# Four places in SBUF for the inner values of an MLP, one for each chunk

## The chip, the cores and the metric

The kernel runs on one core of one Trainium2 chip. The metric is the device time of one execution in microseconds; the kernel before takes 2590.83 us, the median of three runs (2590.58 to 2592.93).

## What is computed

Two transformer-like blocks follow each other on 256 tokens of width 2048, all in float32. The change touches only the MLP at the end of the first block:

```
def sq_relu_mlp(h, w_in, w_out):
    return jnp.square(jax.nn.relu(h @ w_in)) @ w_out
...
    h2 = modulate(rmsnorm(x, norm2_g[i]), sh2, sc2)
    x = x + gt2 * sq_relu_mlp(h2, w_mlp_in[i], w_mlp_out[i])
```

`w_mlp_in` is 2048 x 8192 and `w_mlp_out` is 8192 x 2048. The squared values between the two products (256 tokens x 8192) are called the inner values here. Around the MLP stand a modulation, gated linear attention, a Fourier mixer and output projections before it, and a second block (convolution mixers and a gated MLP) after it.

## The kernel before

**Products in three parts.** Most products are done in TensorE's faster float32 form (`float32r`), with both operands split into a high and a low part: `whi` and `wlo` for the weights, `hh` and `hl` (or `mh` and `ml`) for the activations. One tile of a product is three matmuls: whi by hi (line 289), wlo by hi (line 291), whi by lo (line 293). The weight tile (128 x 128) is the stationary operand, the activations (128 partitions x 256 tokens) are the moving one. This is `feature_piece`. Where the output is wanted with tokens on the partitions, `token_piece` (lines 309, 310, 311) makes the activations stationary and moves 512 columns of `whi` or `wlo`. A few groups use plain float32 from the raw weights (`plain_group`, line 346).

**Weights.** SP's queue streams weights from HBM into the ring `raw` in pieces of 1 MB. ScalarE copies each half of a slot to `whi` (`hi_piece`, line 247), VectorE subtracts to get `wlo` (`lo_piece`, line 257), and TensorE waits for `lo_n` before it uses a piece. `used` frees the `whi`/`wlo` slot again.

**The MLP.** It is done in four chunks of 2048 inner values. A chunk has an in-stage (4 groups of 512 outputs, moving `hh` and `hl`) and an out-stage (4 groups of 512 outputs, moving the inner values `mh` and `ml`). A group is 16 k-tiles x 4 output tiles x 3 matmuls, 192 matmuls of 256 columns, accumulated in one of two PSUM buffers `acc`. After an in-group ScalarE takes the relu of the sums (line 889), VectorE squares (line 1379), ScalarE writes the high part to `mh` (line 891, semaphore `hhi_ok`) and VectorE the low part to `ml` (line 1382, semaphore `hid_ok`). The out-stage waits at its first group for `hid_ok`, inner group by inner group (line 1954). VectorE adds each out-group to `xT` (line 1297). The order is written out by hand: each engine's program runs through the chunks and groups in the same order.

**Where things lie.** Tensors are put one after the other, each starting at a multiple of 32 bytes. By the sizes of the tensors in front of them, `region_h` (with `hh`, `hl`) and `region_a` (with `mh`, `ml` and others that live at other times) start at 32 bytes modulo 128 in each partition. Each k-tile of 256 values is 1024 bytes, so every k-tile of `hh`, `hl`, `mh` and `ml` starts at 32 modulo 128. `oh`, `ol`, `yfh`, `yfl` and `hf` do so too. `whi` starts at 16 and `wlo` at 80 modulo 128 (both are taken 4 words into their tensor), and each 128-column tile keeps that. `dh` and `dl` (the second block's MLP) stand 24 words into `region_a`, at 0 modulo 128.

Of the kernel before, what the change touches and what calls it, by code (L numbers as in the profile page):

```python
# [4 lines left out]
P = 128  # L5
D = 2048
NT = 256
KT = D // P
# [81 lines left out]
def build(nc, ins, out):  # L90
    f32, f32r, u32 = mybir.dt.float32, mybir.dt.float32r, mybir.dt.uint32
    ALU, ACT = mybir.AluOpType, mybir.ActivationFunctionType
# [3 lines left out]
    with ctx:  # L96
# [6 lines left out]
        def overlay(hold, nbytes, *tensors):  # L103

            made = []
            for group in tensors:
# [9 lines left out]
        tmp = sb("tmp", [P, 2, 4 * NT])  # L116
# [23 lines left out]
            "region_h", 32768,  # L140
            [("hh", [P, KT, NT], f32r), ("hl", [P, KT, NT], f32r)],
            [("xN", [P, 2, D], f32), ("gN", [P, 2, D], f32)])
        (ch, cl, sqx, sqc, lab, keb, tq, state, dft, smid, mh, ml, _, dh, dl, hf) = overlay(
            "region_a", 32768 + 512,
            [("ch", [P, KT, NT], f32r), ("cl", [P, KT, NT], f32r)],
            [("sqx", [P, KT, NT], f32), ("sqc", [P, KT, NT], f32)],
# [1 line left out]
             ("state", [P, 2, HEADS, DV], f32), ("dft", [P, 2, DFT_COLS], f32),  # L148
             ("smid", [P, HEADS, DV], f32)],
            [("mh", [P, KT, NT], f32r), ("ml", [P, KT, NT], f32r)],  # L150
            [("behind", [P, 24], f32), ("dh", [P, KT, NT], f32r), ("dl", [P, KT, NT], f32r)],
            [("hf", [P, KT, NT], f32)])

# [33 lines left out]
        mask_w = [con2[:, (4 + d) * P:(5 + d) * P] for d in range(2)]  # L187
        half_w = [con2[:, 6 * P + 2 * d:6 * P + 2 * d + 2] for d in range(2)]
        tiles = lambda ap: ap.rearrange("p (t n) -> p t n", n=NT)
        pcol = lambda name, i=0, n=1: par[:, COL[name] + i:COL[name] + i + n]  # L190


# [490 lines left out]
        def _(act):  # L683
            act.dma_start(par[:, 2 * KT:NPARAM], ins["par"][:, 2 * KT:NPARAM]).then_inc(S["par_in"], 16)
            act.dma_start(con[:, :], ins["con"]).then_inc(S["con_in"], 16)
            st = Turn()
# [194 lines left out]
            for c in range(0, MLP_CHUNKS):  # L881
                for g in range(4):
                    n = 4 * c + g
                    if n:
                        C(st)
                        group_done(act, st)
                    else:
                        act.wait_ge(S["f_used"], 4)
                    nc.scalar.activation(tmp[:, 0, :], acc[g % 2][:, :], ACT.Relu).then_inc(S["relu_ok"], 1)
                    act.wait_ge(S["rsq_ok"], n + 1)  # L890
                    nc.scalar.activation(mh[:, 4 * g:4 * g + 4, :], tiles(tmp[:, 1, :]), ACT.Copy)\
                        .then_inc(S["hhi_ok"], 1)
                for g in range(4):
                    C(st)
                    if c == MLP_CHUNKS - 1:
                        mix_quad(g)
# [166 lines left out]
        def _(dve):  # L1063
# [304 lines left out]
            for c in range(0, MLP_CHUNKS):  # L1368
                for g in range(4):
                    n = 4 * c + g  # L1370
                    if n:
                        C()
                        group_done(dve, st)
                    else:
                        dve.wait_ge(S["f_used"], 4)
                    if c == 0:
                        late_out(dve, st, mp[1], st.e)
                    dve.wait_ge(S["relu_ok"], n + 1)
                    nc.vector.scalar_tensor_tensor(tmp[:, 1, :], acc[g % 2][:, :], 0.0, tmp[:, 0, :],
                                                   ALU.max, ALU.mult).then_inc(S["rsq_ok"], 1)  # L1380
                    dve.wait_ge(S["hhi_ok"], n + 1)
                    nc.vector.tensor_tensor(ml[:, 4 * g:4 * g + 4, :], tiles(tmp[:, 1, :]),
                                            mh[:, 4 * g:4 * g + 4, :].bitcast(f32), ALU.subtract)\
                        .then_inc(S["hid_ok"], 1)
                for g in range(4):
                    if c == MLP_CHUNKS - 1 and g:
                        C(2)
                        mix_lo(g - 1)
                        C(2)
                        mix_sums(g - 1)  # L1390
                        C(4)
                    else:
                        C()
                    group_done(dve, st)
                    if c + g == 0:
                        late_out(dve, st, mp[1], st.e)
                        dve.wait_ge(S["mo_ok"], 24)
                    add_scaled(g % 2, 4 * g, 3 * KT).then_inc(acc_free[g % 2], 1)
# [347 lines left out]
        def _(pe):  # L1746
# [196 lines left out]
            for c in range(0, MLP_CHUNKS):  # L1943
                for g in range(4):
                    if c + g == 0:
                        plain_group(pe, st, 0, hf, 0, n2_plain, lambda s: None, 0)
                    else:
                        mm_feature(pe, st, g % 2, hh, hl, 0, each=n2_ready if c + g == 1 else None,
                                   free=(S["rsq_ok"], 4 * c + g - 1) if g >= 2 else None)
                    if c == 0:  # L1950
                        late_turn(pe, st, mp[1])
                for g in range(4):
                    mm_feature(pe, st, g % 2, mh, ml, 1, free=(S["rsq_ok"], 4 * c + g + 3) if g < 2 else None,
                               ready=(lambda s: pe.wait_ge(S["hid_ok"], 4 * c + s + 1)) if g == 0 else None)
                    if c + g == 0:
                        late_turn(pe, st, mp[1])
                        assert st.t == 16
# [191 lines left out]
```

## Time and profile before

| | |
|---|---|
| median of three timed runs | 2590.83 us |
| the profiled execution | 2592.11 us |
| its span (first to last instruction) | 2590.3 us |
| TensorE matmul busy | 2537.2 us (98%) |
| weight loads busy | 2378.3 us (92%) |
| VectorE, ScalarE busy | 64%, 44% |
| mean granted TensorE clock | 0.993 |

Matmuls are pipelined and overlap in the records: one of 256 columns is drawn 277 to 281 ns long, but the next starts long before it ends. What a matmul costs in a stream is the distance from one start to the next. The views give it: where a line of the source view has n matmuls of one line, first and last start, the distance of the last and first start divided by n-1 is the time of one whole round of three matmuls, called a triple below.

### The profile page before, as it was taken

What the parts mean: (1) busy time and instruction counts of PE and PEld (TensorE: products, weight loads), DVE (VectorE), ACT (ScalarE), POOL (GpSimd) and SP (SyncE); (2) the same over time, 40 slices, a digit from 0 to 9 for tenths busy, and PEclk for the clock granted to TensorE, in tenths of its full rate; (3) what the DMA queues carried; (4) which work ended last, traced back from release to release, by engine and by line L of the source; (5) the groups of instructions that cost most, each with busy time, mean ns of one, the idle gap of its engine ahead of it and who ended that gap; (6) DMA issues with size and microseconds to landing.
All of it is one profiled execution on the core that took longest, in us unless ns stands there. A gap on an engine that the chain in (4) does not pass through costs nothing.

```text
span 2590.3 us, 42561 instructions
## 1 busy us (share of the span) xinstructions
PE 2537.2 (98%) x18912; PEld 2378.3 (92%) x18912; DVE 1658.1 (64%) x1999; ACT 1132.6 (44%) x1299; POOL 11.2 (0%) x24
## 2 busy tenths in 40 slices
PE   6999999999999999999999999999999999999998
PEld 3688799999998999999999999999899889988996
DVE  5366666677785755555555579776677556764775
ACT  3322565544444434434434552054455435543553
POOL 0000000000000000000000000000000000000000
PEclk8999999999999999999999999999999999999999
DMA  9976565588885755555555555454455555555553
GB/s 395 361 254 229 209 218 207 202 296 290 304 292 202 278 190 186 194 192 185 194 193 184 190 183 179 147 179 170 151 185 196 196 194 187 188 195 184 190 183 110
DMA packets 77223, 547.89 MB, mean 212 GB/s; under 512 B 8848, under 2 KB 8976, under 8 KB 12272
## 3 DMA queue, kind: packets, MB, share of 16 engines
q1 hardware_dynamic: 74304, 533.53, 57.7%
q0 software_dynamic: 2448, 11.14, 1.1%
q8 instruction: 148, 2.42, 0.4%
q10 hardware_dynamic: 288, 0.50, 0.1%
q14 instruction: 35, 0.29, 0.0%
HBM read 539.90 MB, written 5.24 MB: 210 GB/s over the span
## 4 chain that ended last, share of the span: by engine, by line
PE 96%; DVE 2%; ACT 1%; DMA 1%; issue 0%; SPq 0%; DVEq 0%; ACTq 0%
PE acc L289 23%; PE acc L293 22%; PE acc L291 22%; PE acc L346 5%; PE acc L309 5%; PE acc L310 5%; PE acc L311 5%; PE mp L376 1%; PE mp L309 1%; PE mp L311 1%; PE mp L310 1%; DMA raw<-in_w_mod 1%; PE mp L435 0%; PE mp L498 0%; DVE macc L420 0%; PE mp L1866 0%
## 5 line engine op out<-in xcount | busy, mean ns | idle before, releaser
L257 DVE TENSOR_TENSOR wlo<-raw,whi 128x1024 fp32r<-128x1024 f32 x773 | 934.9, 1222 | 679.4 <-ACT whi L247 677.7
L247 ACT ACTIVATE whi<-raw 128x1024 fp32r<-128x1024 f32 x773 | 812.1, 1058 | 1171.9 <-PE acc L293 873.3
L293 PE MATMUL acc<-hl,whi 128*128 128x256 f32 x3296 | 922.6, 280 | 0.0
L289 PE MATMUL acc<-hh,whi 128*128 128x256 f32 x3296 | 919.4, 279 | 0.0
L291 PE MATMUL acc<-hh,wlo 128*128 128x256 f32 x3296 | 915.2, 278 | 0.0
L289 PEld LDWEIGHTS acc<-hh,whi 128*128 128x128 f32 x3296 | 622.5, 189 | 4.6 <-issue 3.0
L293 PEld LDWEIGHTS acc<-hl,whi 128*128 128x128 f32 x3296 | 618.8, 188 | 0.0
L291 PEld LDWEIGHTS acc<-hh,wlo 128*128 128x128 f32 x3296 | 616.7, 187 | 0.5
L293 PE MATMUL acc<-ml,whi 128*128 128x256 f32 x1536 | 430.1, 280 | 0.0
L289 PE MATMUL acc<-mh,whi 128*128 128x256 f32 x1536 | 426.4, 278 | 0.0
L291 PE MATMUL acc<-mh,wlo 128*128 128x256 f32 x1536 | 426.4, 278 | 0.0
L289 PEld LDWEIGHTS acc<-mh,whi 128*128 128x128 f32 x1536 | 290.3, 189 | 0.3 <-issue 0.2
L293 PEld LDWEIGHTS acc<-ml,whi 128*128 128x128 f32 x1536 | 288.4, 188 | 0.0
L291 PEld LDWEIGHTS acc<-mh,wlo 128*128 128x128 f32 x1536 | 287.3, 187 | 0.1
L420 DVE SCALAR_TENSOR_TENSOR macc<-raw,csl,macc 128x512 f32<-128x512 f32 x240 | 180.2, 751 | 10.9 <-DMA raw<-in_w_mod 2.9
L346 PE MATMUL acc<-hf,raw 128*128 128x256 f32 x640 | 140.6, 382 | 7.7 <-ACT hf L987 4.1
L346 PEld LDWEIGHTS acc<-hf,raw 128*128 128x128 f32 x640 | 122.5, 192 | 25.3 <-issue 8.4
L310 PE MATMUL acc<-wlo,dh 128*128 128x512 f32 x352 | 139.3, 396 | 0.0
L309 PE MATMUL acc<-whi,dh 128*128 128x512 f32 x352 | 139.0, 395 | 0.0
L311 PE MATMUL acc<-whi,dl 128*128 128x512 f32 x352 | 138.9, 395 | 0.0
L1670 DVE SCALAR_TENSOR_TENSOR up<-um,par,up 128x255 f32<-128x255 f32 (+1 forms) x176 | 73.3, 478 | 25.7 <-ACT up L1010 24.9
L309 PE MATMUL acc<-whi,hh 128*128 128x512 f32 x192 | 80.0, 417 | 2.4 <-DVE hl L547 2.4
(319 smaller groups left out, 2181.4 us busy)
## 6 DMA issues: line engine op xcount, KB each, us to landing
raw<-in_w_in SPq DMA_DIRECT2D x98, 1024.0 KB, 4.9
raw<-in_w_mod SPq DMA_DIRECT2D x96, 1024.0 KB, 5.8
raw<-in_w_up SPq DMA_DIRECT2D x88, 1024.0 KB, 4.9
raw<-in_w_mlp_in SPq DMA_DIRECT2D x64, 1024.0 KB, 4.9
raw<-in_w_mlp_out SPq DMA_DIRECT2D x64, 1024.0 KB, 4.9
raw<-in_w_down SPq DMA_DIRECT2D x44, 1024.0 KB, 4.9
raw<-in_w_out SPq DMA_DIRECT2D x32, 1024.0 KB, 4.9
raw<-in_w_fourier_out SPq DMA_DIRECT2D x8, 1024.0 KB, 5.7
```

Of the source, the lines that this page charges most:

```text
L247: nc.scalar.activation(whi[:, r, :], raw_slot(k)[:, 2 * GC * j:2 * GC * (j + 1)], ACT.Copy)\
L257: nc.vector.tensor_tensor(wlo[:, r, :], raw_slot(k)[:, 2 * GC * j:2 * GC * (j + 1)], whi[:, r, :].bitcast(f32), ALU.subtract).then_inc(S[" ...
L289: nc.tensor.matmul(dst, whi[:, r, cols], hi[:, kt, :], start=begin, stop=False, skip_group_check=True)
L291: nc.tensor.matmul(dst, wlo[:, r, cols], hi[:, kt, :], start=False, stop=False, skip_group_check=True)
L293: last = nc.tensor.matmul(dst, whi[:, r, cols], lo[:, kt, :], start=False, stop=kt == nkt - 1, skip_group_check=True)
L309: nc.tensor.matmul(dst, hi[:, kt, t0:t0 + P], whi[:, r, cols], start=kt == 0, stop=False)
L310: nc.tensor.matmul(dst, hi[:, kt, t0:t0 + P], wlo[:, r, cols], start=False, stop=False)
L311: last = nc.tensor.matmul(dst, lo[:, kt, t0:t0 + P], whi[:, r, cols], start=False, stop=kt == nkt - 1)
L346: last = nc.tensor.matmul(acc[i][:, t * NT:(t + 1) * NT], raw_slot(k)[:, j * GC + t * P:j * GC + (t + 1) * P], h[:, kt, :], start=kt == 0 ...
L376: last = nc.tensor.matmul(rows[32 * t:32 * t + 32, :], cv[:, 4 * s + t, :], raw_slot(k)[:, t * GC:(t + 1) * GC], start=s == 0, stop=s == 3)
L420: ins = nc.vector.scalar_tensor_tensor(macc[:, g % 2, :], part, csl[:, kt:kt + 1], macc[:, g % 2, :], ALU.mult, ALU.add)
L1670: last = nc.vector.scalar_tensor_tensor(y, um[:, t, 0:NT - sh], par[:, ds(col, 1)], y, ALU.mult, ALU.add)
```

## The change

The inner values get a tensor of their own inside the same region, `mhl`, 32 words longer than `mh` and `ml` together. In it each chunk has its own high and low part, starting 24, 16, 4 and 12 words in (chunks 0 to 3). With the region at 32 bytes modulo 128 these are 0, 96, 48 and 80 bytes modulo 128, for the high part and for the low part alike. ScalarE's high copy, VectorE's low subtraction and TensorE's out-stage of chunk c use `inner[c]`. Other users of `mh` and `ml` (the output projections of both mixers) are as before.

```diff
-        (ch, cl, sqx, sqc, lab, keb, tq, state, dft, smid, mh, ml, _, dh, dl, hf) = overlay(
+        (ch, cl, sqx, sqc, lab, keb, tq, state, dft, smid, mh, ml, mhl, _, dh, dl, hf) = overlay(
             "region_a", 32768 + 512,
...
             [("mh", [P, KT, NT], f32r), ("ml", [P, KT, NT], f32r)],
+            [("mhl", [P, 2 * KT * NT + 32], f32r)],
...
+        half = KT * NT
+        inner = [[mhl[:, at + x * half:at + (x + 1) * half].rearrange("p (k n) -> p k n", n=NT) for x in range(2)]
+                 for at in (24, 16, 4, 12)]
...
-                    nc.scalar.activation(mh[:, 4 * g:4 * g + 4, :], tiles(tmp[:, 1, :]), ACT.Copy)\
+                    nc.scalar.activation(inner[c][0][:, 4 * g:4 * g + 4, :], tiles(tmp[:, 1, :]), ACT.Copy)\
                         .then_inc(S["hhi_ok"], 1)
...
-                    nc.vector.tensor_tensor(ml[:, 4 * g:4 * g + 4, :], tiles(tmp[:, 1, :]),
-                                            mh[:, 4 * g:4 * g + 4, :].bitcast(f32), ALU.subtract)\
+                    nc.vector.tensor_tensor(inner[c][1][:, 4 * g:4 * g + 4, :], tiles(tmp[:, 1, :]),
+                                            inner[c][0][:, 4 * g:4 * g + 4, :].bitcast(f32), ALU.subtract)\
                         .then_inc(S["hid_ok"], 1)
...
-                    mm_feature(pe, st, g % 2, mh, ml, 1, free=(S["rsq_ok"], 4 * c + g + 3) if g < 2 else None,
+                    mm_feature(pe, st, g % 2, *inner[c], 1, free=(S["rsq_ok"], 4 * c + g + 3) if g < 2 else None,
                                ready=(lambda s: pe.wait_ge(S["hid_ok"], 4 * c + s + 1)) if g == 0 else None)
```

## Rows read from the trace of the kernel before

**Rows 1.** The page: busy time of the engines, and the granted clock in 40 slices.
```profile
PE 2537.2 (98%) x18912; PEld 2378.3 (92%) x18912; DVE 1658.1 (64%) x1999; ACT 1132.6 (44%) x1299; POOL 11.2 (0%) x24
...
PEclk8999999999999999999999999999999999999999
```

**Rows 2.** Windows: us, busy of each engine, PEclk, DMA share, GB/s. Chunks 0, 1.
```profile
892.50:982.10 89.60, 89.60 (x778) 89.60 (x777) 46.28 (x48) 35.84 (x34) 0.00 (x0) 1.00 0.58 199
982.10:1070.90 88.80, 88.80 (x771) 88.80 (x770) 47.32 (x42) 39.56 (x38) 0.00 (x0) 1.00 0.55 191
892.50:1514.60 622.10, 622.10 (x5386) 622.10 (x5385) 334.55 (x328) 273.82 (x277) 0.00 (x0) 1.00 0.56 191
```

**Rows 3.** Waits, 892.5 to 1514.6 us: who waited for whom, total us, times, longest.
```profile
ACT whi L247 <- PE acc L293: 319.2, 186, 2.7
DVE wlo L257 <- ACT whi L247: 272.3, 173, 5.3
ACT mh L891 <- DVE tmp L1379: 19.7, 13, 1.5
DVE ml L1382 <- ACT mh L891: 14.6, 13, 1.1
```

**Rows 4.** Line 289, out-stage of chunk 1: ns min/median/max, first and last start us.
```profile
L289 PE MATMUL acc<-mh,whi x256: 277/277/278, 1070.9 to 1159.3; 128*128 128x256 f32 x128
```

**Rows 5.** Line 289, in-stage of chunk 1.
```profile
L289 PE MATMUL acc<-hh,whi x256: 277/277/278, 982.2 to 1070.6; 128*128 128x256 f32 x128
```

**Rows 6.** Timeline of ScalarE and VectorE where the inner values of chunk 1 are finished.
```profile
1074.61 1.06 ACT L891 ACTIVATE mh<-tmp 128x1024 fp32r<-128x1024 f32 x1 [1.51 <-DVE tmp L1379]
1075.71 1.23 DVE L1382 TENSOR_TENSOR ml<-tmp,mh 128x1024 fp32r<-128x1024 f32 x1 [1.12 <-ACT mh L891]
```

**Rows 7.** Line 289, four earlier stretches: three from 521 to 560 us, one from 582.
```profile
L289 PE MATMUL acc<-hh,whi x46: 281/281/281, 521.1 to 537.0; 128*128 128x256 f32 x46
L289 PE MATMUL acc<-yfh,whi x32: 281/281/282, 537.3 to 548.3; 128*128 128x256 f32 x32
L289 PE MATMUL acc<-oh,whi x32: 281/281/281, 548.6 to 559.6; 128*128 128x256 f32 x32
L289 PE MATMUL acc<-yfh,whi x32: 277/277/277, 582.4 to 593.1; 128*128 128x256 f32 x32
```

**Rows 8.** Timeline of TensorE, 572.65 to 573.36 us: start, length, line.
```profile
572.65 0.28 PE L289 MATMUL acc<-hh,whi 128*128 128x256 f32 x1
...
573.01 0.28 PE L289 MATMUL acc<-hh,whi 128*128 128x256 f32 x1
...
573.36 0.28 PE L289 MATMUL acc<-hh,whi 128*128 128x256 f32 x1
```

**Rows 9.** Line 309, tokens on the partitions, moving 512 columns: second block, then first.
```profile
L309 PE MATMUL acc<-whi,dh x128: 392/393/397, 2018.3 to 2107.0; 128*128 128x512 f32 x128
L309 PE MATMUL mp<-whi,ch x34: 393/396/399, 152.5 to 197.7; 128*128 128x512 f32 x34
L309 PE MATMUL acc<-whi,hh x33: 393/396/398, 151.8 to 196.3; 128*128 128x512 f32 x33
```

**Rows 10.** Line 361, the low-rank gate: six matmuls a round, 64 stationary columns.
```profile
L361 PE MATMUL acc<-hh,whi x16: 278/279/282, 239.2 to 249.7; 128*64 128x256 f32 x16
```

**Rows 11.** Line 346, plain float32, 1590 to 1650 us.
```profile
L346 PE MATMUL acc<-hf,raw x280: 379/379/380, 1589.7 to 1649.9; 128*128 128x256 f32 x140
```

**Rows 12.** Line 435 in chunk 0's out-stage, two moving columns: timeline, then source view.
```profile
914.72 0.95 PE L435 MATMUL mp<-ones,macc 128*128 128x2 f32 x8
...
L435 PE MATMUL mp<-ones,macc x8: 168/251/252, 914.7 to 915.4; 128*128 128x2 f32 x8
```

## The prediction

> **What bounds the kernel now.** I read the page's busy times first. TensorE's matmuls are busy 98% of the span and the granted clock stands at 9 or more tenths in 39 of 40 slices, so at the upper of its two levels, 2.4 GHz [rows 1]. Then the windows of the MLP: in the out-stage of chunk 0, the in-stage of chunk 1 and the whole stretch from 892.5 to 1514.6 us TensorE is busy for every microsecond, at clock 1.00 [rows 2]. The waits of the same stretch name only ScalarE and VectorE, which wait for TensorE's pieces or for each other; TensorE is not among the waiters [rows 3]. So in the MLP nothing is late. The time is the number of matmuls times the distance of their starts, and only a change of that distance can move the end.
>
> The distance, from the source view: in the out-stage of chunk 1 line 289 starts 256 times from 1070.9 to 1159.3 us, 88.4 / 255 = 346.7 ns for a triple, 115.6 ns for a matmul of 256 columns [rows 4]. In the in-stage before it, with `hh` moving from the same 32 bytes modulo 128, it is 88.4 / 255 = 346.7 ns as well [rows 5]. The out-stages of chunks 2 and 3 show the same to the last digit.
>
> **Part 1: ScalarE's and VectorE's writes go elsewhere.** Four groups in four chunks, 16 writes of each kind, no instruction more or less. The last inner group of chunk 1 is written by ScalarE in 1.06 us from 1074.61 and by VectorE in 1.23 us from 1075.71, so it is ready at 1076.9 [rows 6]. TensorE needs it for the last quarter of the first out-group, 12/16 of 64 triples in: 1070.9 + 48 x 0.3467 = 1087.5 us [rows 4]. That leaves 10.6 us. If these writes took twice as long the cover would still hold, with 8 us left, so I cost them at nothing; both ends of the bound are nothing too, as 2.3 us more is covered and a faster write frees nothing that anyone waits for. If the cover were gone, 2.3 us would stand in each of four chunks, 9 us.
>
> **Part 2: order and waits.** None is added. The place of a chunk overlaps the neighbouring groups of the last one by a few words, but the first write of a chunk follows its own first in-group, and that stands on TensorE's queue behind the last read of the chunk before (in-stage of 88.8 us between them [rows 2]). Nothing on SP's queue moves. Nothing.
>
> **Part 3: where the moving rows start.** This is the only part that can count. It covers 4 chunks x 256 triples = 1024 triples, 355.0 us at 346.7 ns. One nanosecond in a triple is 1.02 us of the kernel. No row shows a 256-column row that starts at 0, 96, 48 or 80, so I bound it.
>
> What a start on other bytes has done so far: in the token stages of the first block the moving operands start at 16 and 80 and the stationary ones at 32: 67 triples of 512 columns, alternating between `acc` and `mp`, start from 151.8 to 197.7 us, 45.9 / 66 = 695.5 ns. In the second block the stationary ones start at 0: 88.7 / 127 = 698.4 ns [rows 9]. So 32 bytes of difference between the operands made at most 2.9 ns in 1536 columns, 0.4%. Per column that is 0.453 ns with 16 and 80 moving, against 346.7 / 768 = 0.451 ns with 32 moving. A start at an odd multiple of 16 is therefore no disaster. Taken over to our 768-column triple, 0.4% is 1.4 ns, 1.5 us in all, of either sign.
>
> The same addresses can run at two distances, though. From 521.1 to 537.0 us line 289 starts 46 times, 15.9 / 45 = 353.3 ns, and this slow pitch goes on through `yfh` and `oh` (11.0 / 31 = 354.8 ns at this rounding), until at 582.4 us `yfh` runs at 10.7 / 31 = 345.2 ns [rows 7]. All of these start at 32. In the drawn length of line 289 the two pitches show as 281 and 277 ns. A stream keeps the pitch that it fell into, through changes of tensor, until something disturbs it. While it changes, a triple can take 573.01 - 572.65 = 360 ns [rows 8]. With the change, the distance in bytes between moving and stationary operands jumps at each of the eight borders between in-stages and out-stages, and each can end in either pitch. The difference is 353.3 - 346.7 = 6.7 ns, 1.7 us for a stage of 256 triples.
>
> Lower end: a matmul with two moving columns has a distance of about 0.112 us, as eight take (0.95 - 0.17) / 7, where 0.17 us is the shortest drawn length, taken for the last; three are 336 ns, a gain of 10.7 ns x 1024 = 10.9 us [rows 12]. Still lower, plain float32 takes 60.2 / 279 = 215.8 ns for 256 columns, two cycles a column; half of it three times is 324 ns, a gain of 23 us [rows 11]. I take the nearer one as the end, since every triple here also loads three weight tiles. That loads are not the whole of it is shown by line 361: six matmuls with half the stationary columns take 10.5 / 15 = 700 ns, 350 for three, no less than ours [rows 10]. Upper end: all four chunks at 353.3 ns, +6.8 us; with the in-stages of chunks 1 to 3 carried along, 7 x 1.7 = 12.0 us; all at 360 ns, +13.6 us.
>
> The value I take is one stage of 256 triples in the slow pitch, +1.7 us: near the 1.5 us that the token rows give, and on the slow side because the present pitch is the faster of the two that the trace shows for this shape.
>
> Here a rule of the Trainium skill speaks. What the row shows is 115.6 ns for a 256-column matmul at full clock [rows 4]. "TensorE: Matmul & The Clock Gate", in "Step-by-step: what each phase is for", has two independent read ports of SBUF, one for the moving operand and one for the weights, so that loading weights takes nothing from the stream, and in "Back-to-back issue gap" a distance of N/2.4 + 2.5 ns. By that rule, as an estimate, the distance were 109.2 ns and no placement could matter: the change would bring 0. The trace is 6.4 ns a matmul above it, so either the ports are not the whole story or this float32 form streams slower by itself.
>
> **The sum.** 0 + 0 + 1.7 us. The profiled execution would go from 2592.11 to 2593.8 us (its span is 2590.3, 1.8 less). It lies 1.3 us above the median of the runs; on the median the forecast is 2590.83 + 1.7 = 2592.5 us.
>
> **Rivals.**
> *Slower by over 0.2%: the slow pitch is what the new places lock into.* Place: the out-stages, and the in-stages behind them. Price 1.7 us for each stage of 256 triples; it decides from the fourth stage on (5.2 us is 3.1 stages), +6.8 us for the four out-stages alone (2597.6) and +12.0 us with the in-stages of chunks 1 to 3 carried along (2602.8). For it: the slow pitch lasted through three tensors, 521.1 to 559.6 us [rows 7], and a jump of addresses eight times over is eight occasions. Against it: the whole MLP runs at the fast pitch now although its chunk 0 is interrupted by line 435 [rows 12], and the slow one is met only in a short part of the kernel.
> *Faster by over 0.2%: a new place runs below 346.7 ns.* The distance is 115.6 ns where loads alone give 112 and columns alone 108, so something costs 3.6 ns or more a matmul; if it is the meeting of the two reads on the same bytes, a place can remove it. All four places at 336 ns: 2579.9. It counts from 5.1 ns a triple over 1024 triples, half of the whole headroom in every chunk, or all of it in two. For it: lengths move with the places in the token stages [rows 9]. Against it: the move there was 0.4% and upward, and line 361 has half the load without being faster [rows 10].
> *The place does nothing*: every stage at 346.7 ns, 2590.8, or the base of the region is not at 32 and other four places are tried; then the same bounds hold. It lies inside my forecast's band.
>
> **Chances.** What a measurement can tell from no change is about 0.2%, 5.2 us: 2585.6 to 2596.0. Forecast and the case of no effect together 0.60 (of this 0.20 for exactly nothing); slow lock of four or more stages 0.29; faster by more than 5.2 us 0.11. The range goes from 2586.5 (inside the faster side of the forecast's band) to 2601, which holds most of the slow rival up to six stages (2601.0) and leaves the ends, some 0.1 on each side.
>
> **What would show it.** Line 289's first and last start in each out-stage: 88.4 us apart for 346.7 ns, 90.1 for 353.3 (drawn lengths 277 and 281 ns), 85.7 for 336. In-stages of `hh` at 88.4 us, unless they carry a slow pitch. Lines 891 and 1382 at 1.06 and 1.23 us; TensorE still waiting for nobody in the stretch. The prediction is wrong if any stage runs at a third distance, below 340 or above 356 ns, or if the writes lengthen by microseconds so that TensorE waits for `ml`.

## The result: 0.5% slower

The changed kernel takes 2606.03 us (median of four runs, 2602.14 to 2606.72) where the kernel before takes 2590.7 us beside it: ratio 1.0051, 95% interval 1.0037 to 1.0066. Forecast were 2592.5 us, with a range from 2586.5 to 2601. Its profiled execution has a span of 2604.9 us, 14.6 more than before.

The instruction counts are the same, and so are the times of the engines that write the inner values. The page of the changed kernel, busy time:

```profile
PE 2551.9 (98%) x18912; PEld 2392.5 (92%) x18912; DVE 1658.4 (64%) x1999; ACT 1132.4 (43%) x1299; POOL 11.2 (0%) x24
```

TensorE is busy 14.7 us longer [rows 1]. The windows (columns as in rows 2) show where: the MLP from the first out-stage on, then up to the plain group of the second block, that group, and the rest.

```profile
892.80:1527.90 635.10, 635.10 (x5387) 635.10 (x5386) 335.34 (x328) 273.69 (x277) 0.00 (x0) 1.00 0.54 188
1527.90:1843.10 315.20, 311.59 (x2290) 299.10 (x2288) 238.70 (x395) 120.83 (x150) 0.00 (x0) 1.00 0.49 172
1843.10:1877.30 34.20, 32.12 (x136) 27.84 (x137) 24.43 (x42) 12.21 (x24) 0.53 (x1) 0.90 0.38 133
1877.30:2604.90 727.60, 715.72 (x5122) 667.88 (x5120) 464.47 (x510) 339.81 (x386) 0.00 (x0) 0.99 0.51 181
```

The same four windows of the kernel before:

```profile
892.50:1514.60 622.10, 622.10 (x5386) 622.10 (x5385) 334.55 (x328) 273.82 (x277) 0.00 (x0) 1.00 0.56 191
1514.60:1829.80 315.20, 311.59 (x2290) 299.04 (x2289) 238.68 (x395) 120.82 (x150) 0.00 (x0) 1.00 0.50 172
1829.80:1862.80 33.00, 30.92 (x136) 26.95 (x137) 24.43 (x42) 12.20 (x24) 0.53 (x1) 0.95 0.39 138
1862.80:2590.30 727.50, 715.72 (x5122) 667.79 (x5120) 464.42 (x510) 339.80 (x386) 0.00 (x0) 1.00 0.51 181
```

The first window took 13.0 us more (635.1 against 622.1) at clock 1.00 and with as many matmuls. The third took 1.2 us more, and there the granted clock is 0.90 in place of 0.95; it is the same code behind a stall of TensorE, so this share is the clock of one execution. Ahead of the first window two differences nearly cancel. The changed kernel comes to the end of the output projections 2.5 us earlier (784.7 against 787.2 us, in stages that the change leaves alone), and the stretch behind, with the plain group of chunk 0's in-stage, takes 2.9 us more, again at a lower granted clock. Before, then changed:

```profile
787.20:823.90 36.70, 31.59 (x148) 27.18 (x146) 20.19 (x29) 17.22 (x30) 0.00 (x0) 1.00 0.49 175
784.70:824.30 39.60, 34.49 (x148) 29.27 (x147) 20.24 (x29) 17.22 (x30) 0.00 (x0) 0.91 0.44 162
```

So of the 14.6 us between the two profiled executions 13.0 are the MLP's, 4.1 are the clock in these two stretches, and 2.5 go the other way. The waits of the first window name nobody new:

```profile
ACT whi L251 <- PE acc L297: 332.0, 198, 2.7
DVE wlo L261 <- ACT whi L251: 284.1, 174, 5.3
ACT mhl L895 <- DVE tmp L1383: 19.6, 13, 1.5
DVE mhl L1386 <- ACT mhl L895: 14.6, 13, 1.1
```

So the distance between matmuls grew. Stage by stage, line 293 (289 of before), ns min/median/max, first and last start; `mhl` is an out-stage, `hh` the in-stage of the next chunk:

```profile
L293 PE MATMUL acc<-mhl,whi x256: 276/281/363, 892.9 to 984.4; 128*128 128x256 f32 x128
...
L293 PE MATMUL acc<-hh,whi x256: 280/281/282, 984.8 to 1074.9; 128*128 128x256 f32 x128
...
L293 PE MATMUL acc<-mhl,whi x256: 275/279/285, 1075.2 to 1164.9; 128*128 128x256 f32 x128
...
L293 PE MATMUL acc<-hh,whi x256: 276/277/282, 1165.2 to 1253.7; 128*128 128x256 f32 x128
...
L293 PE MATMUL acc<-mhl,whi x256: 280/284/285, 1254.0 to 1345.8; 128*128 128x256 f32 x128
...
L293 PE MATMUL acc<-hh,whi x256: 280/281/285, 1346.2 to 1436.3; 128*128 128x256 f32 x128
...
L293 PE MATMUL acc<-mhl,whi x256: 277/281/283, 1436.6 to 1527.6; 128*128 128x256 f32 x128
```

Before, each of them is 88.4 us from first to last start [rows 4, 5], the out-stage of chunk 0 some 0.9 more, as line 435 interrupts it. Now: 91.5 (place 0, chunk 0), 90.1, 89.7 (place 96), 88.5, 91.8 (place 48), 90.1, 91.0 (place 80). In ns a triple: 355.3 (with the 0.9 us taken off), 353.3, 351.8, 347.1, 360.0, 353.3, 356.9. The rows round to 0.1 us, 0.4 ns a triple; the means over the single start times, which the expectations below and the tables use, are 355.6, 353.3, 351.5, 346.7, 360.0, 353.3, 356.7. The sum by these rows: out-stages 2.2 + 1.3 + 3.4 + 2.6 = 9.5 us, in-stages 1.7 + 0.1 + 1.7 = 3.5 us, together 13.0 us.

### The profile page after: what moved, and what is told of

It is laid out like the page before. It is cut to its first block, busy times and chain, and to the rows that moved or that the text cites. A ratio compares the mean times of both kernels' runs of the same rounds, so it can differ in the third digit from the quotient of the medians.

```text
span 2604.9 us, 42561 instructions
## 1 busy us (share of the span) xinstructions
PE 2551.9 (98%) x18912; PEld 2392.5 (92%) x18912; DVE 1658.4 (64%) x1999; ACT 1132.4 (43%) x1299; POOL 11.2 (0%) x24
## 4 chain that ended last, share of the span: by engine, by line
PE 96%; DVE 2%; ACT 1%; issue 0%; DMA 0%; SPq 0%; DVEq 0%; ACTq 0%
PE acc L293 23%; PE acc L297 23%; PE acc L295 22%; PE acc L350 6%; PE acc L313 5%; PE acc L314 5%; PE acc L315 5%; PE mp L380 1%; PE mp L313 1%; PE mp L315 1%; PE mp L314 1%; PE mp L439 0%; PE mp L502 0%; DVE macc L424 0%; PE mp L1870 0%
## 5 line engine op out<-in xcount | busy, mean ns | idle before, releaser
L295 PE MATMUL acc<-mhl,wlo 128*128 128x256 f32 x1024 | 288.3, 282 | 0.0
L293 PE MATMUL acc<-mhl,whi 128*128 128x256 f32 x1024 | 288.1, 281 | 0.0
L297 PE MATMUL acc<-mhl,whi 128*128 128x256 f32 x1024 | 287.2, 280 | 0.0
L297 PEld LDWEIGHTS acc<-mhl,whi 128*128 128x128 f32 x1024 | 194.0, 189 | 0.0
L293 PEld LDWEIGHTS acc<-mhl,whi 128*128 128x128 f32 x1024 | 192.4, 188 | 0.0
L295 PEld LDWEIGHTS acc<-mhl,wlo 128*128 128x128 f32 x1024 | 192.4, 188 | 0.0
L297 PE MATMUL acc<-ml,whi 128*128 128x256 f32 x512 | 143.5, 280 | 0.0
L293 PE MATMUL acc<-mh,whi 128*128 128x256 f32 x512 | 142.8, 279 | 0.1
L295 PE MATMUL acc<-mh,wlo 128*128 128x256 f32 x512 | 142.2, 278 | 0.0
```

The lines of the kernel that those rows point to most:

```text
L293: nc.tensor.matmul(dst, whi[:, r, cols], hi[:, kt, :], start=begin, stop=False, skip_group_check=True)
L295: nc.tensor.matmul(dst, wlo[:, r, cols], hi[:, kt, :], start=False, stop=False, skip_group_check=True)
L297: last = nc.tensor.matmul(dst, whi[:, r, cols], lo[:, kt, :], start=False, stop=kt == nkt - 1, skip_group_check=True)
```

## The experiments

Triples are 256-column matmuls three at a time, as before. Each experiment changes the starting words of the inner values (`at`, 4 bytes each, on top of 32 modulo 128) or what is named. Only e1, e10 and e12 were repeated to compare times; the others are single executions, read by the pitches of their stages. These repeat well: the out-stages of the changed kernel were run in five executions (its own, e8, e9, e13, e17) and are at 355.6, 351.4 to 351.5, 360.0 and 356.7 ns in each. Outside e13 the granted clock is 1.00 in all stages that are read. In chunk 0 line 439 (435 of before) takes 0.9 us out of the out-stage, which is taken off.

### e1: all four chunks at 32 again, in the new tensor

```diff
-                 for at in (24, 16, 4, 12)]
+                 for at in (0, 0, 0, 0)]
```

> Undoes the starting bytes alone: the separate tensor for the inner values stays, but all four chunks start at 32 bytes modulo 128, as before. Theory PLACE (the bytes at which the moving rows start set the pitch of the out-stage, and the in-stage behind may inherit a slow one): all out-stages and in-stages of the MLP back at 346.7 ns a triple, time within 0.1% of the kernel before, 2591 us. Rival TENSOR (the separate tensor, or the overlap between chunks, costs): stays near 2604 to 2606 us with slow stages.

Measured: ratio to the kernel before 0.9999 (0.9989 to 1.0008). All stages are back; the out-stage of chunk 1, then a stretch of the second block in the same execution:

```profile
L293 PE MATMUL acc<-mhl,whi x256: 277/277/277, 1070.4 to 1158.8; 128*128 128x256 f32 x128
...
L293 PE MATMUL acc<-hh,whi x444: 281/281/467, 1863.1 to 2019.8; 128*128 128x256 f32 x148
```

88.4 us again. The bytes are the cause; the separate tensor costs nothing. That the chunks lie staggered in it was undone here together with the places. It costs nothing either by e3, whose chunk 3 at 32 lies staggered against chunk 2 and runs at 346.7 ns, and by e10, where the loss is there without it. The second row shows something else: 156.7 / 443 = 353.7 ns where the kernel before had, in the same code at the same addresses,

```profile
L289 PE MATMUL acc<-hh,whi x448: 277/277/468, 1862.8 to 2018.0; 128*128 128x256 f32 x150
```

155.2 / 447 = 347.2 ns. One pair of places has two pitches, and which one it gets differs between executions, 3 us here. Runs of the kernel before spread from 2587.9 to 2597.7 us in this comparison.

### e2: the same places, other chunks

```diff
+                 for at in (4, 12, 24, 16)]
```

> The same four places given to other chunks: 48, 80, 0 and 96 modulo 128 for chunks 0 to 3 (the changed kernel has 0, 96, 48, 80, with 355.6, 351.5, 360.0 and 356.7 ns a triple). Theory PLACE: the pitches move with the places, 360.0, 356.7, 355.6, 351.5 ns in chunks 0 to 3, and the time is 2602 to 2607 us. Rival HISTORY (what a stage falls into depends on how it is entered, so on the chunk): chunks 0 to 3 keep 355.6, 351.5, 360.0, 356.7, or take new values that belong to no place. For the in-stages: behind 48 and 0 they ran at 353.3 ns and behind 96 at 346.7; by PLACE with inheritance the in-stages of chunks 1 and 3 (behind 48 and 0) are slow and that of chunk 2 (behind 80) fast.

```profile
L293 PE MATMUL acc<-mhl,whi x256: 280/284/364, 892.9 to 985.5; 128*128 128x256 f32 x128
...
L293 PE MATMUL acc<-mhl,whi x256: 278/281/282, 1076.4 to 1167.3; 128*128 128x256 f32 x128
...
L293 PE MATMUL acc<-mhl,whi x256: 276/281/283, 1256.4 to 1347.1; 128*128 128x256 f32 x128
...
L293 PE MATMUL acc<-mhl,whi x256: 276/278/285, 1436.2 to 1525.9; 128*128 128x256 f32 x128
```

92.6 (less 0.9), 90.9, 90.7, 89.7 us: 359.6, 356.5, 355.7, 351.8 ns. The pitches went with the places. HISTORY is out for the out-stages. It is not for the in-stages: behind 48 slow (353.3), behind 80 fast, but behind 0, now in chunk 2, fast (346.7), where it had been slow.

### e3, e6, e7, e4: other places, finer ones, and the two parts apart

e3: `at` = (28, 8, 20, 0), that is 16, 64, 112 and 32.

> The places at multiples of 16 that have not been tried, 16, 64 and 112 modulo 128, for chunks 0 to 2, and 32 for chunk 3. Theory PLACE in its simplest form, only the sixteen-byte steps within 64 count: 16 like 80 (356.7), 64 like 0 (355.6), 112 like 48 (360.0), 32 at 346.7 ns (but 96 at 351.5 already differs from 32, so this form is doubtful). Rival 128: all eight places differ, and one of the three could be below 346.7, down to 336. HISTORY: 32 in chunk 3 need not be at 346.7.

Measured 353.3, 353.3, 353.3 and 346.7 ns, with three different patterns of steps behind the same sum. The simplest form (only 64 bytes count) is out.

```profile
L293 PE MATMUL acc<-mhl,whi x256: 277/280/282, 1076.1 to 1166.2; 128*128 128x256 f32 x128
...
L293 PE MATMUL acc<-mhl,whi x256: 277/277/277, 1434.6 to 1523.0; 128*128 128x256 f32 x128
```

e6: `at` = (1, 2, 31, 30), that is 36, 40, 28 and 24.

> Places between multiples of 16: 36, 40, 28 and 24 modulo 128 in chunks 0 to 3, high and low alike, whi and wlo as in the changed kernel. If what counts is 16-byte lines that are read whole, 36 and 40 cross one line more in a row than 32 does and need not be near 346.7; I expect 36 and 40 between 346.7 and 360 and 28 and 24 (in the lines of 16) between 346.7 and 357. If single bytes count steadily, 36 and 28 are within 3 ns of 346.7. A place below 346.7 would make a version faster than both kernels.

Measured 361.7, 356.0, 351.1 and 361.6 ns: four bytes up from the best place cost more than any multiple of 16 does (15.0 ns), four bytes the other way 4.4 ns. 36 and 24 lie above what I expected.

```profile
L293 PE MATMUL acc<-mhl,whi x256: 278/284/364, 893.5 to 986.6; 128*128 128x256 f32 x128
...
L293 PE MATMUL acc<-mhl,whi x256: 277/278/280, 1257.3 to 1346.8; 128*128 128x256 f32 x128
...
L293 PE MATMUL acc<-mhl,whi x256: 280/283/286, 1436.0 to 1528.2; 128*128 128x256 f32 x128
```

e4 and e7 give the high and the low part places of their own (shown is e4; e7 has the high part at word 0 and the low part at 28, 8, 16 and 20):

```diff
-            [("mhl", [P, 2 * KT * NT + 32], f32r)],
+            [("mhl", [P, 2 * KT * NT + 64], f32r)],
...
+        inner = [[mhl[:, a:a + half].rearrange("p (k n) -> p k n", n=NT) for a in (at[0], half + 32 + at[1])]
+                 for at in ((4, 0), (0, 4), (24, 0), (0, 24))]
```

> High and low part at different places: chunk 0 high 48 low 32, chunk 1 high 32 low 48, chunk 2 high 0 low 32, chunk 3 high 32 low 0. In a triple two matmuls move the high part (lines 289 and 291 of before), one the low part. If each matmul pays for its own place, high alone at 48 costs two thirds of the 13.3 ns (355.6) and low alone one third (351.1); for 0, 8.9 ns split as 352.6 and 349.7. Rival PAIR (what counts is the jump from one moving row to the next, or the whole triple as one locked cycle): values that don't add up, above 360 or below 346.7 possible.

Measured 357.7, 356.6, 353.3 and 350.0 ns. For place 0 the parts nearly add up (6.6 + 3.3 = 9.9 against 8.9 together), for 48 they don't (11.0 + 9.9 = 20.9 against 13.3): the low part, one matmul of three, costs nearly as much as the high one.

> High part at 32 in all chunks, low part alone at 16, 64, 96 and 112 modulo 128. So far a low part alone at 48 gave 356.6 and at 0 gave 350.0 ns a triple, the high part alone at those 357.7 and 353.3. If each matmul paid for its own place, the low part (one matmul of three) would cost a third of what both together did: 348.9, 348.9, 348.3, 348.9 ns. By PAIR (the triple is one cycle that locks as a whole) values off that by several ns, of either sign; below 346.7 is possible.

Measured 352.0 to 353.3 (two pitches in one stage), 350.0, 353.3 and 346.7 ns, where thirds would be 348.9, 348.9, 348.3, 348.9. A price for each matmul by itself is out. Both forms of PAIR, the jump from one moving row to the next and the triple as one cycle, are left; these runs don't separate them. The low part at 112 costs nothing. Nothing is below 346.7.

### e5, e11, e14: the weights moved as well

```diff
-        whi = sb("whi", [P, 8 * GC + 16], f32r)[:, 4:8 * GC + 4].rearrange("p (r n) -> p r n", r=4)
-        wlo = sb("wlo", [P, 8 * GC + 16], f32r)[:, 4:8 * GC + 4].rearrange("p (r n) -> p r n", r=4)
+        whi = sb("whi", [P, 8 * GC + 16], f32r)[:, 8:8 * GC + 8].rearrange("p (r n) -> p r n", r=4)
+        wlo = sb("wlo", [P, 8 * GC + 16], f32r)[:, 8:8 * GC + 8].rearrange("p (r n) -> p r n", r=4)
...
+                 for at in (4, 8, 28, 0)]
```

> whi and wlo move on by 16 bytes, to 32 and 96 modulo 128, in the whole kernel; the inner values start at 48, 64, 16 and 32 in chunks 0 to 3; hh stays at 32. Known so far, with whi at 16 and wlo at 80: moving 0, 16, 32, 48, 64, 80, 96, 112 gave 355.6, 353.3, 346.7, 360.0, 353.3, 356.7, 351.5, 353.3 ns a triple. Theory RELATIVE (what counts is the distance in bytes between the moving row and the weight tile): each place behaves as the one 16 bytes before it did, so 346.7, 360.0, 355.6, 353.3 in the out-stages and 353.3 in the in-stages of hh. Rival ABSOLUTE (the moving row's own place counts, the weights' place not): 360.0, 353.3, 353.3, 346.7, and hh at 346.7. By RELATIVE the whole kernel slows: some 4000 triples of hh by 6.7 ns are 20 to 25 us, about 2620 us or more; by ABSOLUTE about 2600 us.

```profile
L293 PE MATMUL acc<-mhl,whi x256: 280/281/367, 898.7 to 990.1; 128*128 128x256 f32 x128
...
L293 PE MATMUL acc<-hh,whi x256: 281/281/286, 990.5 to 1080.6; 128*128 128x256 f32 x128
...
L293 PE MATMUL acc<-mhl,whi x256: 276/276/283, 1261.8 to 1350.3; 128*128 128x256 f32 x128
```

Measured 354.9, 353.3, 346.7, 353.3 ns and hh at 353.3 throughout, 2625.6 us in one run. Both theories fail: now 16 is the good place, and 32 never runs at 346.7 ns in this execution.

e11 puts the weights at 0 and 64 (slices from word 0) and the inner values at 48, 16, 64, 112 (`at` = (4, 28, 8, 20)).

> whi at 0 and wlo at 64 modulo 128, inner values at 48, 16, 64 and 112 in chunks 0 to 3, hh at 32. The shift to 32 and 96 gave 354.9, 353.3, 346.7, 353.3 ns for inner values at 48, 64, 16, 32: neither the distance nor the place alone. Theory XOR (the pitch belongs to the exclusive or of the two places, as if a memory bank were chosen by mixed address bits; it fits eight and four values, 48 against 16 as 354.9 to 355.6): 48 gives 346.7, 16 gives 355.6, 64 gives 356.7, 112 gives 351.5, and hh at 32 gives 360.0 in the whole kernel, 55 us and more slower. Theory RELATIVE, which failed once: 48 like 64 at 353.3, 16 like 32 at 346.7, 64 like 80 at 356.7, 112 like 0 at 355.6, hh like 48 at 360.0. A third possibility is that a place of the weights has a table of its own: hh other than 360.0.

Measured 353.3, 358.7, 353.3, 346.7 ns, hh 353.3. XOR fell with its first new table, RELATIVE again. Places 16 and 112:

```profile
L293 PE MATMUL acc<-mhl,whi x256: 278/283/287, 1080.7 to 1172.1; 128*128 128x256 f32 x128
...
L293 PE MATMUL acc<-mhl,whi x256: 276/276/279, 1443.8 to 1532.3; 128*128 128x256 f32 x128
```

e14 puts them at 48 and 112 (slices from word 12) and the inner values at 0, 32, 64, 80 (`at` = (24, 0, 8, 12)).

> whi at 48 and wlo at 112 modulo 128, inner values at 0, 32, 64 and 80 in chunks 0 to 3. Theory STEP32 (moving everything by 32 bytes changes nothing, moving it by 16 does; between weights at 0 and at 32 two of three comparable places agreed and one was 3.8 ns off): the table of weights at 16, moved by 32, gives 351.5 (as 96), 355.6 (as 0), 346.7 (as 32) and 360.0 for 80 (as 48), hh at 32 355.6 or 353.3. Rival OWN (each place of the weights has its own table): other values, above all no 346.7 at 64.

```profile
L293 PE MATMUL acc<-mhl,whi x256: 276/278/367, 902.3 to 992.8; 128*128 128x256 f32 x128
...
L293 PE MATMUL acc<-mhl,whi x256: 280/281/281, 1265.8 to 1355.9; 128*128 128x256 f32 x128
...
L293 PE MATMUL acc<-mhl,whi x256: 279/284/285, 1447.1 to 1538.9; 128*128 128x256 f32 x128
```

Measured 351.4, 355.0, 353.3, 360.0 ns against 351.5, 355.6, 346.7, 360.0 of STEP32. The one miss, 64, has the drawn lengths (281) and the sum of the slow twin of the 346.7 pitch. All values, ns a triple, high and low part alike:

| moving rows start at | whi 0, wlo 64 | whi 16, wlo 80 | whi 32, wlo 96 | whi 48, wlo 112 |
|---|---|---|---|---|
| 0 | | 355.6 | | 351.4 |
| 16 | 358.7 | 353.3 | 346.7 | |
| 32 | 353.3 | 346.7 or 353.3 | 353.3 | 355.0 |
| 48 | 353.3 | 360.0 | 354.9 | |
| 64 | 353.3 | 353.3 | 353.3 | 353.3 |
| 80 | | 356.7 | | 360.0 |
| 96 | | 351.5 | | |
| 112 | 346.7 | 353.3 | | |

Moving everything by 32 bytes mostly keeps a value (seven comparable pairs: four equal to 0.1 ns, two off by 0.6 and 3.8 ns, one in a slow twin). Moving everything by 16 does not. A 353.3 that is drawn 281 ns long may also be the slow twin of a place whose fast pitch no stage met; 16 with `whi` at 16 and 32 with `whi` at 32 are of this kind, so whether these two differ from 346.7 for good is open.

The pitch belongs to the pair of places, twin or not: 16 runs at 346.7 ns with `whi` at 32, and `whi` at 0 gives 346.7 with the moving rows at 112, but the two together, 16 with `whi` at 0, give 358.7. Moving the weights also moves where ScalarE and VectorE write them. Momentary meetings with these writes don't make the pitch: in the in-stage of chunk 1 of the kernel before all 255 distances between starts are 346 or 347 ns, while VectorE is busy for 47.32 and ScalarE for 39.56 of 88.8 us [rows 2, 5].

### e15, e16: wlo alone moved

e15: `wlo` from word 12 (112), e16: from word 8 (96), `whi` stays at 16; `at` = (24, 16, 8, 0) in both, that is 0, 96, 64, 32.

> wlo alone moved from 80 to 112, whi stays at 16; inner values at 0, 96, 64 and 32, hh at 32. If only the weight tile that is loaded while a row moves matters, the triple changes in one of its three matmuls and the pitch by a third of what a place can do (up to 4 ns); hh at 346.7 to 351 ns. If the triple is one cycle, anything from 346.7 to 360. A value below 346.7 would be a version better than both kernels; I give it 1 in 10.

> As the run before with wlo at 96 instead of 112 (now an even multiple of 16, while whi stays at an odd one). Same expectations: hh at 346.7 to 351 ns if loads count singly; the four places between 346.7 and 360; below 346.7 with 1 in 10.

```profile
L293 PE MATMUL acc<-mhl,whi x256: 279/279/279, 1448.6 to 1540.4; 128*128 128x256 f32 x128
```

That is inner place 32 with `wlo` at 112: 91.8 / 255 = 360.0 ns, and hh runs there at 360.0 or 353.3, in stretches of chunk 0 and of the second block at 350.0; the inner values at 96 and 64 run at 355.6 and 353.3, those at 0 at 356.7 ahead of line 439's break and at 360.0 behind it, so a break can also lead into a slower pitch. With `wlo` at 96 hh runs at 351.1, 353.3 or 360.0, the inner values at 355.6, 356.6, 350.0 and 351.1. Moving one of the two weight tiles is enough to move the pitch over its whole width, and a stream can have more than two steady pitches. The runs took 2634.5 and 2617.6 us. Nothing below 346.7 was found in the 41 combinations of places run.

### e10: the size, all chunks at 48

```diff
+                 for at in (4, 4, 4, 4)]
```

> All four chunks at 48 modulo 128, the slowest of the eight places, as a test of the size. Theory PLACE with inheritance: four out-stages at 360.0 ns, 4 x 256 x 13.3 ns = 13.7 us; the in-stages of chunks 1 to 3 behind a place of 48 at 353.3 ns, 3 x 1.7 = 5.1 us; the start of the next stage up to 0.3 us: 18.8 to 19.1 us over the kernel before of the same chip, ratio 1.0073. Without inheritance 13.7 us, 1.0053. If the loss were a matter of having several different places, it would be gone: 1.000.

Measured 1.0081 (1.0065 to 1.0097), with four out-stages at 360.0 and three in-stages at 353.3 ns. PLACE with inheritance gives 1.0073 and lies in the interval; without inheritance it would be 1.0053, which does not.

```profile
L293 PE MATMUL acc<-hh,whi x256: 281/281/285, 983.6 to 1073.7; 128*128 128x256 f32 x128
...
L293 PE MATMUL acc<-mhl,whi x256: 279/284/285, 1074.0 to 1165.8; 128*128 128x256 f32 x128
```

### e8, e9, e13, e17: can a slow in-stage be freed?

All four put matmuls with two moving columns into the in-stages of the changed kernel:

```diff
+            def between(n):
+                def run(k0):
+                    for _ in range(n if k0 == 2 else 0):
+                        nc.tensor.matmul(mp[1][:, 0:2], ones[:, :], ones[:, 0:2], start=True, stop=True)
+                return run
...
-                        mm_feature(pe, st, g % 2, hh, hl, 0, each=n2_ready if c + g == 1 else None,
+                        mm_feature(pe, st, g % 2, hh, hl, 0, each=n2_ready if c + g == 1 else short.get(c) if g == 0 else None,
```

> The changed kernel with a short break in the in-stages: after the first eight triples of the in-stage of chunk 1, eight matmuls with two moving columns, and at the same point of chunk 3's two of them. Theory CARRY (the in-stages of hh behind the places 0 and 48 ran at 353.3 ns because the stream kept a slow pitch that it fell into at the border; a disturbance lets it fall into the fast one, as the breaks of line 435 do in the out-stage of chunk 0): both in-stages run at 346.7 ns after the break, 248 x 6.7 = 1.65 us less each, against about 1.0 us for eight extra matmuls and 0.3 us for two. The out-stages keep their pitches. Rival FIXED (an in-stage's pitch follows from where the inner values around it lie): they stay at 353.3 ns. I am less sure of two matmuls than of eight.

The eight of chunk 1 were not issued (the condition in front takes that group), the two of chunk 3 left the stream at 353.3 ns. e9 issues eight in both (`each=between(8) if g == 0 and c in (1, 3)`).

> The changed kernel with eight matmuls of two moving columns after the first eight triples of the in-stages of chunks 1 and 3. In the run before, two such matmuls in chunk 3 moved nothing (353.3 ns before and behind them), and the ones meant for chunk 1 were not issued. Theory CARRY: after eight of them both in-stages run at 346.7 ns, as streams of hh behind line 435's eight do. Rival FIXED: 353.3 ns in both, as with two. The out-stages 355.6, 351.5, 360.0 and 356.7 ns in either case.

```profile
988.13 1.84 PE L1950 MATMUL mp<-ones 128*128 128x2 f32 x16
...
L293 PE MATMUL acc<-hh,whi x248: 280/281/363, 989.8 to 1077.2; 128*128 128x256 f32 x124
...
L293 PE MATMUL acc<-hh,whi x248: 280/281/363, 1353.0 to 1440.3; 128*128 128x256 f32 x124
```

Still 87.4 / 247 = 353.8 ns. CARRY in the form I gave it, any disturbance will do, failed. The first line, from the timeline, shows what such a break is: these matmuls are plain float32, and one that is issued stands as two records. Eight add 1.7 us from start to start of line 293, not the expected 1.0, and two (e8) 0.36 us. Line 435's eight records [rows 12] are four matmuls, 0.9 us. e13 tries six lengths ahead of the in-groups 1 to 3 (`k0 == 0`; counts 1, 3, 5 in chunk 1 and 8, 12, 16 in chunk 3).

> The changed kernel with breaks of matmuls of two columns ahead of the in-groups 1, 2 and 3: 1, 3 and 5 of them in chunk 1, 8, 12 and 16 in chunk 3. Theory PHASE (a stream of hh has two steady pitches, 346.7 and 353.3 ns, and which one it takes behind a break depends on the break's length): some of the six counts free the stream and some do not, and 8 at a group border may differ from 8 in the middle. Rival FIXED: all groups of both stages stay at 353.3 ns. If all groups behind the first border are at 346.7 ns, it is the group border that matters, not the length.

```profile
L293 PE MATMUL acc<-hh,whi x64: 277/277/365, 1008.8 to 1030.7; 128*128 128x256 f32 x64
...
L293 PE MATMUL acc<-hh,whi x63: 280/281/363, 1372.5 to 1394.5; 128*128 128x256 f32 x63
```

Behind one short matmul the stream runs at 346.7 ns, behind eight at 353.3, behind twelve and sixteen at 346.7. Three and five met a stream that was fast already, and behind twelve and sixteen the granted clock fell as well (last section), so these four are no clean test of the length. e17 repeats the one, in both chunks (`each=between(1) if c in (1, 3) and g == 1`).

> The changed kernel with one matmul of two columns ahead of in-group 1 of chunk 1 and of chunk 3. Theory PHASE (the pitch behind a break depends on the break's length; one short matmul freed chunk 1's stream in the run before): both streams at 353.3 ns up to the break and at 346.7 ns behind it, 192 x 6.7 ns = 1.3 us less in each. Rival CHANCE: the one of chunk 3, or both, stay at 353.3 ns.

```profile
L293 PE MATMUL acc<-hh,whi x64: 281/281/282, 982.0 to 1004.2; 128*128 128x256 f32 x64
...
L293 PE MATMUL acc<-hh,whi x192: 277/277/365, 1004.7 to 1071.1; 128*128 128x256 f32 x192
...
L293 PE MATMUL acc<-hh,whi x64: 281/281/285, 1342.3 to 1364.6; 128*128 128x256 f32 x64
...
L293 PE MATMUL acc<-hh,whi x192: 277/277/365, 1365.1 to 1431.4; 128*128 128x256 f32 x192
```

Both freed: 66.4 / 191 = 347.6 ns including the change-over, 281 becomes 277. The slow in-stages are the slow twin of the same addresses, entered at the border. One short matmul ahead of a group left it in three of three tries (e13, e17); ahead of the same group of chunk 3 eight did not (e13). So far PHASE holds. How the pitch depends on the length is not mapped: two were tried only in the middle of a group.

### e12: the kernel before with such a break

```diff
-                            mm_feature(pe, st, v, hh, hl, 1, ready=split if c + p == 0 else None)
+                            mm_feature(pe, st, v, hh, hl, 1, ready=split if c + p == 0 else None,
+                                       each=between(8) if (c, p, v) == (0, 1, 0) else None)
```

> The kernel before with one addition: eight matmuls of two columns in the first block of stages of the second MLP, after its first in-group and eight triples. That stretch (447 triples from 1863 us) ran at 346.7 ns in some executions and at 353.3 in others, 3.0 us. If a break lets a slow stream fall into the fast pitch, this version has no slow executions there: faster than before by up to 2.5 us where before is slow and slower by 1.0 us where it is fast, on the median between 0.1% faster and the same. If a break does nothing, 1.0 us slower.

Measured 1.0008 (1.0000 to 1.0017), median 2594.4 against 2592.9 us: the break costs its time, 1.7 us or 0.07% by e9, and gives nothing back that the runs can show. It is a weak test: in the profiled execution the stream ran at 346.7 ns ahead of the break as well as behind it, and eight freed no stream in e9 or e13. No version that was run is faster than the kernel before.

## Why the prediction was wrong, by its own steps

- *What bounds the kernel*: right. TensorE waits for nobody in the MLP, before and after; the whole difference is the distance of its starts.
- *Part 1, the writes*: right. Lines 895 and 1386 take 1.06 and 1.23 us as lines 891 and 1382 did [rows 6], and the waits between ScalarE and VectorE are the same to 0.1 us.
- *Part 2, waits and overlap*: right, 0. TensorE waits for nobody from 892.8 to 1527.9 us, and e1, which keeps the separate tensor, is at 0.9999.
- *Part 3, where the moving rows start*: this is the step that failed, in two numbers. It took 1.7 us, one stage in the slow pitch. Measured are 9.5 us in the out-stages (8.9, 4.8, 13.3 and 10.0 ns a triple for the places 0, 96, 48 and 80) and 3.5 us in the in-stages, 13.0 in all. And it ended the range at six stages of 353.3 ns, 2601.0 us, as if the new places could only choose between the two pitches that the trace shows at place 32. Its own bound of all stages at 360 ns, +13.6 us, stayed outside the range. They have pitches of their own, three of four above 353.3. The text named what would refute it, a stage above 356 ns, and two stages are.
- *The sizing row was the wrong neighbour.* The token stages [rows 9] differ by 32 bytes between the operands and by 0.4%. They move 512 columns for one load of weights; our shape moves 256. In our shape 32 bytes make up to 13 ns in 347, 4% (`wlo` in e15; 12 ns for the moving rows in the table). From two pairs of places I read that "a start at an odd multiple of 16 is no disaster", which is untrue here (48 and 80). Whether the token shape is less sensitive or its two pairs happened to lie close, no run shows.
- *The step from one stream to the next*: right as a mechanism and priced right, but it stood in the rival and not in the sum: the in-stages of chunks 1 and 3 at 353.3 ns, 1.7 us each. That a disturbance frees a stream was too simple: one short matmul at a group border did, two and eight did not.
- *The slower rival* had place and mechanism for the 3.5 us and, for the out-stages, the right place with a price of 6.8 us in place of 9.5. With 29 in 100 it was the second case, where no row gave a reason to prefer the smaller one: the present place runs at the lowest pitch that any stretch of this shape shows, and four new ones are four draws that could hardly be better.
- *The faster rival*: none of the 41 combinations of places is below 346.7 ns. The bound by short matmuls (336 ns) is not approached. The two rows behind the lower bounds were read by records: a plain float32 matmul leaves two (64 in a plain group stand as x128, line 346 from 1831.9 us), so 215.8 ns [rows 11] is half of a matmul of 256 columns, which takes 431.6 ns, and the eight of rows 12 are four. No term of the sum rests on this.
- *The rule of the two read ports*, "TensorE: Matmul & The Clock Gate", "Step-by-step: what each phase is for", in the Trainium skill: the trace disagrees with what the prediction drew from it, that no placement could matter. The pitch belongs to the pair of places (346.7 and 346.7 ns apart, 358.7 together, e5 and e11), and moving `wlo` alone by 32 bytes turned 346.7 into 360.0 ns (e15). TensorE loads weights and moves rows at once for all of 622.10 us [rows 2]; that the two disturb each other fits this, but which structure makes them do so no run shows. The formula N/2.4 + 2.5 is called the gap of an isolated matmul in "Back-to-back issue gap" of the same page of the Trainium skill, and for a stream with weight loads both operations are said to set the distance; so 115.6 against 109.2 ns spoke neither for nor against the ports.

What stays open: the rule behind the table. Its places are worked out from the sizes of the tensors, no run reads an address; the distances between the places are sure, the zero they are counted from is not. Distance, place and exclusive or each failed; that 32 bytes for everything keep most values and 16 do not is a regularity with one exception of 3.8 ns, not an explanation. Open is too why a stream enters the slow twin behind some places (0 in chunk 0, 48, 16, 36, 24) and not behind others (96, 80, 64, 112, 40, 28, and 0 in chunk 2).

## What to carry to other kernels

In a stream like this one, `float32r` matmuls of 256 columns that TensorE never leaves, the bytes at which operands start are a parameter worth 4%; it is read in one execution, as the first and last start of each stage, and several places can be tried at once, one a stage. Bound such a change by the measured spread of the same shape, and where the present value is the lowest seen, expect a new one to be worse. A spread of a few tenths of a per cent between executions can in part be one stretch in the slow twin of its pitch: compare stage by stage before a cause is sought elsewhere.

## What the runs showed of the hardware that I had not expected

- One pair of addresses has two steady pitches, 346.7 and 353.3 ns (drawn lengths 277 and 281), kept for hundreds of matmuls and left, three times of three, behind a single matmul of two columns.
- Four bytes count: the moving rows at 28, 32, 36 and 40 modulo 128 run at 351.1, 346.7, 361.7 and 356.0 ns.
- Behind twelve short matmuls (e13) the granted clock fell: windows ahead of them, behind them, and later.

```profile
1372.40:1394.80 22.40, 22.40 (x191) 22.40 (x192) 11.67 (x10) 9.03 (x9) 0.00 (x0) 1.00 0.47 162
1397.70:1401.70 4.00, 4.00 (x22) 4.00 (x22) 2.34 (x2) 1.06 (x1) 0.00 (x0) 0.57 0.75 252
1401.70:1410.00 8.30, 8.30 (x74) 8.30 (x73) 3.34 (x3) 3.19 (x3) 0.00 (x0) 1.00 0.18 46
```

A mean of 0.57 is mostly the lower level, 1.2 GHz: 22 matmuls in 4 us where 35 fit. Behind sixteen it is 0.57 over 4 us as well; behind eight it stayed at 1.00 (first row). TensorE had been issuing all the while, but matmuls of two columns.
